# Expert weights as four rows to a partition, in 2 MB transfers, for thirteen of sixteen pairs of experts

## The chip, the cores and the metric

The kernel runs on one core of one Trainium2 chip. The metric is the device time of one execution in microseconds; lower is better.

## The reference

One step of a decoder layer in float32, for 256 prompt tokens and 8 sample tokens (264 in all), each 1024 wide: a gated recurrent mixer and a pooling mixer, then a mixture of 32 experts of which each token takes four, then a gated embedding and a final norm. The change touches the experts alone:

```
for each token: its 4 best experts e (router logits), with softmax weights
    gate = min(x @ w_gate[e] + b_gate[e], 7)          w_gate[e]: 1024 x 1024 float32, 4 MB
    up   = clip(x @ w_up[e] + b_up[e], -7, 7)         w_up[e]:   the same
    act  = (up + 1) * gate * sigmoid(1.702 * gate)
    y   += weight * (act @ w_down[e] + b_down[e])     w_down[e]: the same
```

All 32 experts are computed, so 96 matrices of 4 MB, 403 MB, are read from DRAM once.

## The kernel before

The core keeps everything in one SBUF tensor, `arena` (128 partitions), and uses the eight PSUM banks, `bank`. First come the mixers and the router (about 300 us), then the experts, two at a time in sixteen pairs, then the embedding gate and the output.

**Weights.** A matrix is read in four transfers of 1 MiB, called pieces here. Piece g holds rows 256g to 256g+255; `parts` (L425) gives partition p the rows 256g+2p and 256g+2p+1, which lie next to each other in DRAM, 8 KB in one run. A pair has 24 pieces: for each of gate, up and down (m = 0, 1, 2) and each step g = 0 to 3, one for each of the two experts. They go through a ring of 16 places in SBUF (`gran`). SyncE's queue (SP) issues them in the order in which they are used (`load_experts`, L445; the first two pairs in `load_first`, L437 and L439). Before each issue it waits on `s_used`, which TensorE raises when a piece is used up. TensorE waits for a piece on the semaphore of its place (`granules`).

**Rows of activations.** Since partition p holds rows 2p and 2p+1 of its 256, the other operand of a product must hold the same features on its partitions. Every second column is picked when the activations are turned: `every_other(k)` gives a slice with step 2, and with it `gather` (L1048, the prompt tokens), `gather_samples` (L1058) and `turn_half` (L1066) read their stationary operand. The gain of the norm is laid out the same way in `gffn`, made from a transposed copy of `g_ffn` at the job ("gf",), L753.

**Order of one pair on TensorE** (`pair`): the last gate step (g = 3); the up biases (L1158); the four up steps (L1142); the gather of the first half of the next pair's tokens (L1048, L1058); the turn of the activations (L1066) and of the combining matrix (L1213); the four down steps (L1142); the gather of the second half; the gate biases and the first three gate steps of the next pair (L1172); the mix of this pair's output into the token order (L1224). A step is 8 products of 128 rows by 64 columns with 512 moving columns. Each float32 product appears as two instructions in the trace, a transpose as one. So a step is 16 instructions, and a pair has 32 at L1048, 16 at L1058 and 8 at L1066. Pairs are counted from 0. In pair 14 the projection of the embeddings (L1077) is put between the up steps.

VectorE and ScalarE clip, gate and copy between these steps. The loop over pairs 2 to 13 is unrolled by two.

Of the kernel before, what the change touches and what calls it, by code (L numbers as in the profile page):

```python
# [14 lines left out]
P = 128  # L15
# [7 lines left out]
KD = D // P  # L23
# [86 lines left out]
def build(nc, x_prompt, x_sample, p_prompt, p_sample, state_hgrn, state_pool, g_mix, w_in,  # L110
# [14 lines left out]
    with ExitStack() as ctx:  # L125
# [40 lines left out]
        gain_rows = view(OG + 3 * P, P)  # L166
        lbt = view(take(32), 32)
# [5 lines left out]
        gffn = view(take(KD), KD)  # L173
        power = view(take(1), 1)
# [12 lines left out]
        def heads(start):  # L187
# [35 lines left out]
            "p (j n) -> p j n", j=2) for g in range(RING)]  # L223
        early = {7: view(TMP, GRAN).rearrange("p (j n) -> p j n", j=2),
# [80 lines left out]
        s_gr = [sem(f"granule{g}_loaded") for g in range(RING)]  # L305
        s_half = [sem(f"first_half_of_last_piece{n}_loaded") for n in range(2)]
# [104 lines left out]

        block = ctx.enter_context(nc.Block())
# [3 lines left out]
        def _(sp):  # L416
# [8 lines left out]
            parts = [w.rearrange("o e (g p j) n -> (o e) g p j n", j=2, p=P) for w in (w_gate, w_up, w_down)]  # L425
            ple = w_ple_gate[0].rearrange("(g j p) n -> g p j n", j=2, p=P)
# [14 lines left out]
            def load_experts(i, e, split=False):  # L441

                for at_ in range(2 * NGRAN * PER - (2 if split else 0)):
                    sp.wait_ge(s_used, 2 * NGRAN * i + at_ + 3)
                    sp.dma_start(gran[at_ % RING], source(at_, e)).then_inc(s_gr[at_ % RING], 16)  # L445
# [189 lines left out]
        def _(pe):  # L635
# [408 lines left out]
            def gather(ks, signal=None):  # L1044

                for k in ks:
                    for t in range(2):
                        ins = pe.matmul(XG[k // 4][:, (k % 4) * P:(k % 4 + 1) * P], h2[:, t, every_other(k)], oh[:, t, :],  # L1048
                                        start=(k % 4 == 0 and t == 0), stop=False, skip_group_check=True)
                        if signal and k % 4 == 0 and t == 0:  # L1050
                            ins.then_inc(signal, 1)

            def gather_samples(halves_=range(2)):
# [9 lines left out]
            def turn_half(out, src, c, signal=None):  # L1063
# [18 lines left out]
            def pair(i0, n, opening=False, second=False, last=False, project_tiles=False, alone=False):  # L1082

                i = i0 + n

                def granules(m, g, n=n):

                    for one in range(2):
                        at_ = 2 * NGRAN * n + 8 * m + 2 * g + one
                        if isinstance(i0, int) and i0 == 0 and at_ in early:  # L1090
                            pe.wait_ge(s_early[at_], 16)
                            yield early[at_]
                        elif isinstance(i0, int) and i0 == 0:
                            place = place_of(at_)
                            pe.wait_ge(s_gr[place], 16 if at_ <= 16 else 16 * ((at_ - 19) // RING + 2))
                            yield gran[place]
                        else:
                            pe.wait_ge(s_gr[at_ % RING], i0 * (16 * 2 * NGRAN // RING) + 16 * ((at_ - 19) // RING + 2))
                            yield gran[at_ % RING]

                def products(m, out, src, first, steps=range(4)):

                    for g in steps:
# [30 lines left out]
                        for j in range(2):  # L1134
# [3 lines left out]
                            for c in range(2):  # L1138
                                if halved and j == 1 and c == 1:
                                    ins.then_inc(s_yh, 1)  # L1140
                                for one in range(2):
# [4 lines left out]
                                    if m == 1 and k == 0 and c == 0 and one == 0:  # L1146
                                        ins.then_inc(s_used, 1)
                                    if j == 1 and c == 1 and not (g == 3 and one == 1):
                                        ins.then_inc(s_used, 1)
# [11 lines left out]
                def next_gate_steps():  # L1161

                    biases(range(2), i + 2)
                    for g in range(3):
                        if g != 1:
                            pe.wait_ge(s_xe, 2 * i + 3 + g // 2)
                        w = list(granules(0, g, n + 1))
# [1014 lines left out]
```

## Time and profile before

| | |
|---|---|
| device time, median of 3 runs | 1276.72 us (1275.2 to 1278.67) |
| the profiled execution's own time | 1274.7 us |
| its span, first to last instruction | 1273.0 us |
| mean granted TensorE clock | 0.998 of full speed |
| TensorE busy | 1242.8 us, 98% |
| weight loads of TensorE busy | 614.1 us, 48% |
| VectorE, ScalarE, GpSimd busy | 340.0, 172.5, 48.6 us |
| read from DRAM | 454.41 MB |

A busy engine is one that executes an instruction; TensorE's weight loads are counted apart from its products, since the two overlap. All views below are of one profiled execution, with times from the start of its span. A wait or a chain is put together from semaphore events.

### The profile page before, as it was taken

What the parts mean: (1) busy time and instruction counts of PE and PEld (TensorE: products, weight loads), DVE (VectorE), ACT (ScalarE), POOL (GpSimd) and SP (SyncE); (2) the same over time, 40 slices, a digit from 0 to 9 for tenths busy, and PEclk for the clock granted to TensorE, in tenths of its full rate; (3) what the DMA queues carried; (4) which work ended last, traced back from release to release, by engine and by line L of the source; (5) the groups of instructions that cost most, each with busy time, mean ns of one, the idle gap of its engine ahead of it and who ended that gap; (6) DMA issues with size and microseconds to landing.
All of it is one profiled execution on the core that took longest, in us unless ns stands there. A gap on an engine that the chain in (4) does not pass through costs nothing.

```text
span 1273.0 us, 15848 instructions
## 1 busy us (share of the span) xinstructions
PE 1242.8 (98%) x6326; PEld 614.1 (48%) x6326; DVE 340.0 (27%) x685; ACT 172.5 (14%) x434; POOL 48.6 (4%) x129
## 2 busy tenths in 40 slices
PE   9999999999999999999999999999999999999996
PEld 7857888855434344343434433333334343434343
DVE  3155445423131213122121303122121212121224
ACT  3136204011101010000001000000000010101013
POOL 2221000200000000000000000000000000000001
PEclk9999999999999999999999999999999999999999
DMA  9947713698999999999999999999999999999961
GB/s 347 287 143 261 273 67 97 238 354 355 417 409 415 422 421 422 420 422 421 422 422 422 422 422 422 422 422 422 422 421 422 422 422 422 422 422 420 421 241 36
DMA packets 79782, 460.98 MB, mean 362 GB/s; under 512 B 8158, under 2 KB 9235, under 8 KB 30842
## 3 DMA queue, kind: packets, MB, share of 16 engines
q1 hardware_dynamic: 74512, 445.18, 85.5%
q0 software_dynamic: 3280, 10.75, 2.7%
q10 hardware_dynamic: 1946, 4.43, 1.0%
q8 instruction: 31, 0.51, 0.2%
q14 instruction: 13, 0.11, 0.0%
HBM read 454.41 MB, written 6.39 MB: 362 GB/s over the span
## 4 chain that ended last, share of the span: by engine, by line
PE 78%; DMA 15%; SPq 5%; DVE 1%; issue 1%; ACT 0%; POOLq 0%; POOL 0%; DVEq 0%
PE bank L1142 29%; DMA arena<-in_w_gate_dram 10%; PE bank L1172 9%; PE bank L704 9%; PE bank L1224 5%; SPq L445 5%; PE bank L746 4%; PE bank L1048 3%; PE bank L685 2%; DMA arena<-in_w_down_dram 2%; DMA arena<-in_w_up_dram 2%; PE bank L1158 2%; PE bank L1058 2%; PE bank L1281 1%; PE bank L1299 1%; PE bank L896 1%
## 5 line engine op out<-in xcount | busy, mean ns | idle before, releaser
L1142 PE MATMUL bank<-arena 128*64 128x512 f32 x2352 | 520.3, 595 | 14.1 <-DMA arena<-in_w_up_dram 7.9
L1142 PEld LDWEIGHTS bank<-arena 128*64 128x64 f32 x2352 | 166.3, 137 | 349.3 <-issue 347.8
L1172 PE MATMUL bank<-arena 128*64 128x512 f32 x720 | 159.1, 595 | 1.0 <-DMA arena<-in_w_gate_dram 1.0
L2061 DVE TENSOR_TENSOR arena<-bank,arena 128x512 f32<-128x512 f32 (+1 forms) x92 | 59.0, 683 | 244.9 <-PE bank L1224 244.6
L704 PE MATMUL bank<-arena 128*128 128x264 f32 x512 | 115.9, 388 | 0.0
L704 PEld LDWEIGHTS bank<-arena 128*128 128x128 f32 x512 | 96.8, 190 | 16.6 <-issue 0.2
L1172 PEld LDWEIGHTS bank<-arena 128*64 128x64 f32 x720 | 51.1, 137 | 107.1 <-issue 107.1
L1048 PEld LDWEIGHTS bank<-arena 128*128 128x128 f32 x512 | 62.8, 196 | 25.4 <-issue 25.2
L1224 PE MATMUL bank<-arena 128*128 128x512 f32 (+1 forms) x192 | 75.0, 602 | 0.0
L2043 DVE TENSOR_SCALAR arena<-bank 128x512 f32<-128x512 f32 x32 | 20.6, 686 | 193.3 <-PE bank L1142 193.3
L2054 DVE COPY arena<-bank 128x512 f32<-128x512 f32 x16 | 11.1, 692 | 223.2 <-PE bank L1142 223.2
L1535 ACT ACTIVATE arena<-bank,arena 128x128 f32<-128x128 f32 x120 | 34.2, 368 | 265.0 <-PE bank L1058 265.0
L1048 PE MATMUL bank<-arena 128*128 128x128 f32 x512 | 68.9, 288 | 0.0
L746 PE MATMUL bank<-arena 128*128 128x264 f32 x256 | 57.2, 387 | 0.9 <-ACT arena L1414 0.9
L1547 ACT ACTIVATE arena<-arena 128x1024 f32<-128x1024 f32 x16 | 16.9, 1057 | 298.0 <-DVE arena L2023 298.0
L746 PEld LDWEIGHTS bank<-arena 128*128 128x128 f32 x256 | 48.6, 190 | 9.2 <-ACT arena L1414 1.0
L1224 PEld LDWEIGHTS bank<-arena 128*128 128x128 f32 (+1 forms) x192 | 24.5, 155 | 47.7 <-issue 47.1
L1158 PE MATMUL bank<-arena 32*128 32x512 f32 x128 | 40.4, 627 | 0.0
L1058 PE MATMUL bank<-arena 8*128 8x128 f32 x256 | 38.6, 290 | 0.0
L1567 ACT ACTIVATE arena<-bank 128x512 f32<-128x512 f32 x15 | 9.0, 597 | 210.3 <-PE bank L1142 210.3
L615 POOL TENSOR_SCALAR arena<-arena 128x1 f32<-128x1 f32 (+1 forms) x3 | 0.7, 217 | 944.7 <-ACT arena L1588 944.7
L1058 PEld LDWEIGHTS bank<-arena 8*128 8x128 f32 x256 | 32.5, 191 | 3.8
(264 smaller groups left out, 762.9 us busy)
## 6 DMA issues: line engine op xcount, KB each, us to landing
arena<-in_w_gate_dram SPq DMA_DIRECT2D x128, 1024.0 KB, 25.8
arena<-in_w_up_dram SPq DMA_DIRECT2D x128, 1024.0 KB, 26.0
arena<-in_w_down_dram SPq DMA_DIRECT2D x126, 1024.0 KB, 26.1
arena<-in_w_in_dram SPq DMA_DIRECT2D x14, 2048.0 KB, 11.0
out_dram<-arena POOLq DMA_DIRECT2D x9, 512.0 KB, 6.9
arena<-in_state_hgrn_dram POOLq DMA_DIRECT2D x8, 512.0 KB, 8.1
arena<-sample_values ACTq DMA_DIRECT2D x8, 512.0 KB, 8.9
arena<-in_w_out_dram SPq DMA_DIRECT2D x4, 1024.0 KB, 8.0
```

The costliest lines, as they stand in the source:

```text
L445: sp.dma_start(gran[at_ % RING], source(at_, e)).then_inc(s_gr[at_ % RING], 16)
L685: ins = pe.matmul(job_bank(name)[:, :], hT[:, k, toks(t)], w[:, k, :], start=(k == 0), stop=(k == KD - 1))
L704: ins = pe.matmul(job_bank(name)[:, 0:T], w[:, k, (c % 4) * P:(c % 4 + 1) * P], hT[:, k, :], start=(k == 0), stop=(k == KD - 1))
L746: ins = pe.matmul(job_bank((kind, h))[:, 0:T], w_slot[c % NSLOT][:, k, (h % 4) * P:(h % 4 + 1) * P], hT[:, k, :], start=(k == 0), stop=(k ...
L1048: ins = pe.matmul(XG[k // 4][:, (k % 4) * P:(k % 4 + 1) * P], h2[:, t, every_other(k)], oh[:, t, :], start=(k % 4 == 0 and t == 0), stop=F ...
L1058: ins = pe.matmul(XG[c][:, k * P:(k + 1) * P], h2[rows, 2, every_other(4 * c + k)], oh[rows, 2, :], start=False, stop=True, skip_group_che ...
L1142: ins = pe.matmul(out[c][hp(one), :], src[:, k * P + CAP * one:k * P + CAP * one + CAP], w[one][:, j, halves(c)], start=(first and k == 0) ...
L1158: pe.matmul((GATE + UP)[r][:, :], esel[rows], bias_gu[rows], start=True, stop=False, tile_position=(r * NE, 0))
L1172: ins = pe.matmul(GATE[c][hp(one), :], xT_e[:, k * P + CAP * one:k * P + CAP * one + CAP], w[one][:, j, halves(c)], start=False, stop=False)
L1224: return pe.matmul(out, comb[:, toks(t)], y_sb[:, halves(c)], start=True, stop=True)
L1535: ins = act.activation(xT_e[:, k * P:(k + 1) * P], bank[6 + c][:, (k % 4) * P:(k % 4 + 1) * P], ACT.Copy, scale=gffn[:, k:k + 1])
L2061: ins = dve.tensor_tensor(xs, src, xs, ALU.add)
```

## The change

For pairs 2 to 14 (the third to the fifteenth), a matrix is read in two transfers of 2 MiB. Partition p gets the rows 512G+4p to 512G+4p+3, 16 KB in one run of DRAM. Such a transfer fills two neighbouring places of the ring (`twin`), so there are eight of them, each with its own semaphore. The stream keeps its total and the order of matrices; within a matrix it is now half G of one expert, half G of the other. A transfer is issued when both places are used up, and TensorE raises `s_used` by 2 after every second step of an expert. Steps g = 0 and 1 read the two halves of one transfer, and so do g = 2 and 3.

The features on a partition change with it: for these pairs the gathers and the turn of the activations use a step of 4. The gain is kept a second time in that layout (`gffn_4`, from four more small transposes, one more copy and one more small load), and ScalarE scales with it. Pairs 0, 1 and 15 stay as they were; pair 1 gathers for pair 2 with step 4, pair 14 for pair 15 with step 2.

```diff
+        twin = [view(HG + (g - 4) * 2 * GRAN if 4 <= g < 6 else R + (g if g < 4 else g - 2) * 2 * GRAN, 2 * GRAN).rearrange(
+            "p (j n) -> p j n", j=4) for g in range(RING // 2)]
...
+            parts_4 = [w.rearrange("o e (g p j) n -> (o e) g p j n", j=4, p=P) for w in (w_gate, w_up, w_down)]
...
+            def load_twins(i, e, count):
+
+                for at_ in range(count):
+                    sp.wait_ge(s_used, 2 * NGRAN * i + 2 * at_ + 4)
+                    sp.dma_start(twin[at_ % (RING // 2)], parts_4[at_ // 4 % 3][e + 2 * (at_ // 12) + at_ % 2, at_ // 2 % 2])\
+                      .then_inc(s_twin[at_ % (RING // 2)], 16)
...
             with sp.Fori(1, PAIRS // PER - 1) as q:
-                load_experts(PER * q, 2 * PER * q)
-            load_experts(PAIRS - PER, NE - 2 * PER, split=True)
+                load_twins(PER * q, 2 * PER * q, NGRAN * PER)
+            load_twins(PAIRS - PER, NE - 2 * PER, NGRAN)
+            load_experts(PAIRS - PER, NE - 2 * PER, range(2 * NGRAN, 2 * NGRAN * PER - 2))
...
-            pe.wait_ge(ld["gffnr"], 16)
+            pe.wait_ge(ld["gffnr"], 32)
             begin(("gf",))
             for j in range(2):
                 pe.transpose(bank[5][:, 4 * j:4 * j + 4], gfin_rows[0:4, j:2 * P:2], ident[0:4, 0:4])
+            for j in range(4):
+                pe.transpose(bank[5][:, 32 + 2 * j:34 + 2 * j], gfin_rows_4[0:2, j:4 * P:4], ident[0:2, 0:2])
...
-            def every_other(k):
-                first = 2 * P * (k // 2) + k % 2
-                return slice(first, first + 2 * P - 1, 2)
+            def every_other(k, j=2):
+                first = j * P * (k // j) + k % j
+                return slice(first, first + j * (P - 1) + 1, j)
...
-                        ins = pe.matmul(XG[k // 4][:, (k % 4) * P:(k % 4 + 1) * P], h2[:, t, every_other(k)], oh[:, t, :],
+                        ins = pe.matmul(XG[k // 4][:, (k % 4) * P:(k % 4 + 1) * P], h2[:, t, every_other(k, j)], oh[:, t, :],
...
-                        ins = pe.matmul(XG[c][:, k * P:(k + 1) * P], h2[rows, 2, every_other(4 * c + k)], oh[rows, 2, :],
+                        ins = pe.matmul(XG[c][:, k * P:(k + 1) * P], h2[rows, 2, every_other(4 * c + k, j)], oh[rows, 2, :],
...
-                    ins = pe.transpose(out[c][:, j * P:(j + 1) * P], src[:, every_other(k)], ident)
+                    ins = pe.transpose(out[c][:, j * P:(j + 1) * P], src[:, every_other(k, step_)], ident)
...
+                        if twins:
+                            at_ = NGRAN * n + 4 * m + g // 2 * 2 + one
+                            pe.wait_ge(s_twin[at_ % (RING // 2)], i0 * (16 * 2 * NGRAN // RING) - 48 + 16 * (at_ // (RING // 2) + 1))
+                            yield twin[at_ % (RING // 2)][:, 2 * (g % 2):2 * (g % 2) + 2]
...
-                                    if j == 1 and c == 1 and not (g == 3 and one == 1):
-                                        ins.then_inc(s_used, 1)
+                                    if j == 1 and c == 1 and not (g == 3 and one == 1) and (g % 2 or not twins):
+                                        ins.then_inc(s_used, n_used)
...
-                    gather(range(4), s_used)
-                    gather_samples((0,))
+                    gather(range(4), s_used, n_used, next_apart)
+                    gather_samples((0,), next_apart)
...
-                    turn_half(AT, act_sb, c, s_used if last else None).then_inc(s_aT, 1)
+                    turn_half(AT, act_sb, c, s_used if last else None, rows_apart).then_inc(s_aT, 1)
...
             with pe.Fori(1, PAIRS // PER - 1) as q:
                 for n in range(PER):
-                    pair(PER * q, n)
-            pair(PAIRS - PER, 0, project_tiles=True)
+                    pair(PER * q, n, twins=True, next_twins=True)
+            pair(PAIRS - PER, 0, project_tiles=True, twins=True)
```

## Rows read from the trace of the kernel before

**Rows 1.** The page: busy shares, and the span in 40 equal slices.
```profile
PE 1242.8 (98%) x6326; PEld 614.1 (48%) x6326; DVE 340.0 (27%) x685; ACT 172.5 (14%) x434; POOL 48.6 (4%) x129
...
GB/s 347 287 143 261 273 67 97 238 354 355 417 409 415 422 421 422 420 422 421 422 422 422 422 422 422 422 422 422 422 421 422 422 422 422 422 422 420 421 241 36
```

**Rows 2.** The chain in order of time, one pair: start us, us, what.
```profile
600.01 1.06 PE bank L1158 x4
...
614.96 2.08 PE bank L1048 x16
617.04 1.14 PE bank L1058 x8
618.17 1.15 PE bank L1066 x8
...
637.66 10.45 PE bank L1172 x48
648.11 4.59 PE bank L1224 x12
652.70 3.58 PE bank L1142 x16
656.29 1.06 PE bank L1158 x4
```

**Rows 3.** The chain, marks of pairs 2, 8, 9 and 14, and the last wait.
```profile
431.19 1.06 PE bank L1158 x4
...
768.84 1.06 PE bank L1158 x4
...
828.30 1.06 PE bank L1158 x4
...
1114.64 3.65 PE bank L1172 x16
...
1126.47 1.06 PE bank L1158 x4
```

**Rows 4.** The waits of TensorE: us in total, times, longest us.
```profile
PE bank L1142 <- DMA arena<-in_w_up_dram: 7.9, 6, 1.3
PE bank L1142 <- DMA arena<-in_w_down_dram: 6.2, 6, 1.0
```

**Rows 5.** DMA packets of 16:24, 1218:1226 and 900:1000 us.
```profile
DMA packets 1673, 3.16 MB, mean 395 GB/s; under 512 B 149, under 2 KB 153, under 8 KB 1672
...
DMA packets 853, 3.28 MB, mean 410 GB/s; under 512 B 52, under 2 KB 52, under 8 KB 853
...
DMA packets 5796, 42.21 MB, mean 422 GB/s; under 512 B 644, under 2 KB 644, under 8 KB 644
```

**Rows 6.** The page, DMA issues: count, KB each, median us to landing.
```profile
arena<-in_w_gate_dram SPq DMA_DIRECT2D x128, 1024.0 KB, 25.8
```

**Rows 7.** Weight loads by form: count | busy us, mean ns of one | idle.
```profile
L704 PEld LDWEIGHTS bank<-arena 128*128 128x128 f32 x512 | 96.8, 190 | 16.6 <-issue 0.2
L1048 PEld LDWEIGHTS bank<-arena 128*128 128x128 f32 x512 | 62.8, 196 | 25.4 <-issue 25.2 <-DVE arena L1906 0.3
...
L1066 PEld LDWEIGHTS bank<-arena 128*128 128x128 f32 x128 | 16.5, 208 | 4.1 <-DVE arena L2049 2.3
...
L646 PEld LDWEIGHTS bank<-arena 128*128 128x128 f32 x32 | 3.5, 140 | 0.1
...
L1224 PEld LDWEIGHTS bank<-arena 128*8 128x8 f32 x64 | 1.7, 87 | 12.1 <-issue 12.1
```

**Rows 8.** Timeline of TensorE, 226.5 to 229 us: start us, us.
```profile
226.91 1.97 PE L646 MATMUL bank<-arena 128*128 128x128 f32 x16
228.71 0.61 PE L704 MATMUL bank<-arena 128*128 128x264 f32 x2
```

**Rows 9.** VectorE by form; L1945 and L1995 reduce with 128-byte steps.
```profile
L1945 DVE TENSOR_REDUCE arena<-arena 128x32 f32<-128x128 f32 x3 | 1.0, 372 | 0.1
L1995 DVE TENSOR_REDUCE arena<-arena 128x96 f32<-128x384 f32 x1 | 0.8, 820 | 0.0
...
L1994 DVE TENSOR_TENSOR arena<-arena 128x384 f32<-128x384 f32 x1 | 0.6, 557 | 0.0
```

More of the change, by code:

```diff
@@ L166, in build @@
         gain_rows = view(OG + 3 * P, P)
+        gfin_rows_4 = view(OG + 4 * P, 4 * P)
         lbt = view(take(32), 32)
@@ L173, in build @@
         gffn = view(take(KD), KD)
+        gffn_4 = view(take(KD), KD)
         power = view(take(1), 1)
@@ L305, in build @@
         s_gr = [sem(f"granule{g}_loaded") for g in range(RING)]
+        s_twin = [sem(f"two_places{g}_loaded") for g in range(RING // 2)]
         s_half = [sem(f"first_half_of_last_piece{n}_loaded") for n in range(2)]
@@ L410, in place_of @@
             return (at_ + (3 if at_ < 7 else 2)) % RING if at_ <= 16 else at_ % RING
+        first_loads = [sum(place_of(a) == g for a in range(2 * NGRAN * PER) if a not in early) for g in range(RING)]
+        last_loads = [sum(a % RING == g for a in range(2 * NGRAN, 2 * NGRAN * PER)) for g in range(RING)]
         block = ctx.enter_context(nc.Block())
@@ L439, in load_first, with load_experts @@
                     sp.dma_start(gran[place_of(at_)], source(at_, 0)).then_inc(s_gr[place_of(at_)], 16)
-            def load_experts(i, e, split=False):
-                for at_ in range(2 * NGRAN * PER - (2 if split else 0)):
+            def load_twins(i, e, count):
[3 more added lines that the diff above has]
+                      .then_inc(s_twin[at_ % (RING // 2)], 16)
+            def load_experts(i, e, ats=range(2 * NGRAN * PER)):
+                for at_ in ats:
                     sp.wait_ge(s_used, 2 * NGRAN * i + at_ + 3)
@@ L1080, in project, with pair, granules @@
                             fill_done(ins, ("pp" + r, t, j))
-            def pair(i0, n, opening=False, second=False, last=False, project_tiles=False, alone=False):
+            def pair(i0, n, opening=False, second=False, last=False, project_tiles=False, alone=False, twins=False,
+                     next_twins=False):
                 i = i0 + n
-                def granules(m, g, n=n):
+                rows_apart, next_apart = (4 if twins else 2), (4 if next_twins else 2)
+                n_used = 2 if twins else 1
+                def granules(m, g, n=n, twins=twins):
                     for one in range(2):
                         at_ = 2 * NGRAN * n + 8 * m + 2 * g + one
-                        if isinstance(i0, int) and i0 == 0 and at_ in early:
+                        if twins:
+                            at_ = NGRAN * n + 4 * m + g // 2 * 2 + one
+                            pe.wait_ge(s_twin[at_ % (RING // 2)], i0 * (16 * 2 * NGRAN // RING) - 48 + 16 * (at_ // (RING // 2) + 1))
+                            yield twin[at_ % (RING // 2)][:, 2 * (g % 2):2 * (g % 2) + 2]
+                        elif isinstance(i0, int) and i0 == 0 and at_ in early:
                             pe.wait_ge(s_early[at_], 16)
@@ L1166, in next_gate_steps @@
                             pe.wait_ge(s_xe, 2 * i + 3 + g // 2)
-                        w = list(granules(0, g, n + 1))
+                        w = list(granules(0, g, n + 1, next_twins))
                         for j in range(2):
@@ L1174, in next_gate_steps @@
                                                     w[one][:, j, halves(c)], start=False, stop=False)
-                                    if j == 1 and c == 1:
-                                        ins.then_inc(s_used, 1)
+                                    if j == 1 and c == 1 and (g % 2 or not next_twins):
+                                        ins.then_inc(s_used, 2 if next_twins else 1)
                 if opening:
@@ L1217, in pair @@
                 if not last:
-                    gather(range(4, KD), s_used)
-                    gather_samples((1,))
+                    gather(range(4, KD), s_used, n_used, next_apart)
+                    gather_samples((1,), next_apart)
                 def mix_half(t, c):
@@ L1331, in _ @@
             pair(0, 0, opening=True)
-            pair(0, 1, second=True)
+            pair(0, 1, second=True, next_twins=True)
             with pe.Fori(1, PAIRS // PER - 1) as q:
                 for n in range(PER):
-                    pair(PER * q, n)
-            pair(PAIRS - PER, 0, project_tiles=True)
+                    pair(PER * q, n, twins=True, next_twins=True)
+            pair(PAIRS - PER, 0, project_tiles=True, twins=True)
             pair(PAIRS - PER, 1, last=True)
@@ L1528, in _, with rows_in @@
             act.activation(exw, exw, ACT.Exp).then_inc(s_rta, 1)
-            def rows_in(i, c):
+            def rows_in(i, c, gain=gffn):
                 act.wait_ge(s_xg, 2 * i + c + 1)
@@ L1535, in rows_in @@
                     ins = act.activation(xT_e[:, k * P:(k + 1) * P], bank[6 + c][:, (k % 4) * P:(k % 4 + 1) * P], ACT.Copy,
-                                         scale=gffn[:, k:k + 1])
+                                         scale=gain[:, k:k + 1])
                 ins.then_inc(s_xe, 1)
@@ L1541, in projected, with pair @@
                 copy_out(name, pps[t][lanes(t), cols(t, n)], piece(name))
-            def pair(i, first=False, second=False, last=False, project_tiles=False):
+            def pair(i, first=False, second=False, last=False, project_tiles=False, next_gain=gffn):
                 if first:
@@ L1558, in pair @@
                 if not last:
-                    rows_in(i + 1, 0)
+                    rows_in(i + 1, 0, next_gain)
                 act.wait_ge(s_cT, i + 1)
@@ L1631, in _ @@
             pair(0, first=True)
-            pair(1, second=True)
+            pair(1, second=True, next_gain=gffn_4)
             with act.Fori(2, PAIRS - PER) as i:
-                pair(i)
+                pair(i, next_gain=gffn_4)
             pair(PAIRS - PER, project_tiles=True)
```

21 lines of the change are left out of this document (14 added, 7 removed).

## The prediction, before the changed kernel was run

> **What bounds the kernel now.** I read the page first: TensorE is busy for 98% of the span, and the DMA engines move 422 GB/s in nearly every slice from the fourteenth to the thirty-eighth [rows 1]. Two things that look full mean that the chain in order of time has to say which one is late. The reader is to see two regimes in it. In a pair in the middle of the span the chain holds TensorE work only, and from one pair's up biases (L1158) to the next it is 656.29 - 600.01 = 56.28 us [rows 2]. Those same marks stand at 431.19 for pair 2 and 768.84 for pair 8, six pairs at 56.27 us; then at 828.30, a step of 59.46, and so on to 1126.47 for pair 14 [rows 3]. A pair reads 24 pieces of 1 MiB, 25.17 MB; at 422 GB/s that is 59.63 us, so a piece lasts 2.485 us. DMA was always 3.4 us a pair slower than TensorE, TensorE ate up the lead that the loads had, and from pair 7 on it waits for weights. Had TensorE never waited, the twelve pairs from 431.19 to 1126.47 would take 12 x 56.27 = 675.2 us instead of 695.3: waits for weights cost 20.1 us in all. The list of waits names 14.1 us of them [rows 4]; the rest lies in gaps that it gives to nobody, and I use the distances of the marks. The last such wait ends at 1114.64, at the third gate step of pair 14 [rows 3], which needs that pair's first six pieces, number 342 of the stream counted from the first. From there to the end only TensorE and what follows it counts. So faster DMA can win at most 20.1 us, and every microsecond added to TensorE's 56.27 costs nothing while it is under 3.4 us a pair, and all of it above.
>
> **The change, part by part.** There are thirteen pairs (2 to 14) with 2 MiB transfers.
>
> *Longer rows.* A partition's run in DRAM grows from 8 KB to 16 KB. No row of before has a 16 KB run issued by SP, so I extrapolate: in three stretches the engines moved almost only 2 KB, 4 KB and 8 KB packets, at 395, 410 and 422 GB/s [rows 5]. Per packet and engine that is 2048 x 16 / 395 = 83 ns, 160 ns and 310.6 ns: about 75.4 ns per 2 KB and 9 ns that does not grow. A 16 KB packet then takes 310.6 + 301.6 = 612 ns, which is 428 GB/s and 2.449 us for 1 MiB, 0.036 us less than now. Between piece 48, the first of pair 2, and the 344 that the critical step will need lie 296 pieces: -10.7 us, if the loads set the end. The bounds are nothing, if a 16 KB run is cut in two, and 296 x 0.072 = -21.4 us if the whole fixed part went (301.6 ns for 8 KB, 2.413 us a piece), of which the loop can take up 20.1.
>
> *Coarser transfers.* The third gate step now waits for both experts' second transfers, so for eight pieces of its pair and not six: +2 x 2.485 = +5.0 us wherever the loads set the end. Places come free later too: the third gate step's pieces are now held over the mix (L1224, 4.59 us) and the last gate step (3.6 us), and the first of every two steps 3.5 us longer [rows 2]. That cannot empty the queue: a transfer lands 25.8 us after its issue now [rows 6], over ten pieces of backlog; less 8.2 + 3.5 us of later release and 5.0 us for the transfer itself, 9 us stay. I cost it at nothing; were that backlog not there, each later release would show as a gap in the loads.
>
> *Rows of activations four apart.* The weights of a partition are now rows 4p to 4p+3, so the gather (L1048, L1058) and the turn of the activations (L1066) take their stationary operand with a step of four floats, 16 bytes, instead of two. This is the part that is on TensorE's path in every pair: 32 + 16 + 8 instructions, with no cover but TensorE's own. What they cost now [rows 2]: 2.08 / 16 = 130 ns each, 142, and 1.15 / 8 = 144. Is a load bound by reading? The rows of weight loads [rows 7]: 8 columns take 87 ns, 128 adjacent columns 190 in a product and 140 in a transpose, with a step of two 196 and 208. So a column costs (140 - 87) / 120 = 0.44 ns when four share 16 bytes, and 1.01 ns when two do: 1.8 to 2.0 ns per 16 bytes either way. The spacing shows it: sixteen transposes of adjacent columns start 226.91 and are over by 228.71, 112 ns apart [rows 8], those with a step of two 144. With 196 and 208 ns loads the instructions come 130 and 144 ns apart, so the spacing is the load less some 65 ns. No TensorE row has a step of 16 bytes. VectorE has: its reduction over 128-byte steps takes 372 ns for 128 elements and 820 for 384, 1.75 ns an element, where an operation on 384 adjacent ones takes 557 [rows 9]. From below the price is nothing: if reading goes in units of 8 bytes, a step of two already pays one unit per column, and VectorE's 820 ns may be the work of closing 96 sums. From above it is 2.02 ns a column, twice the 1.01 of the transposes. I take twice the step of a strided product load, 2 x (196 - 87) / 120 = 1.82 ns, near the 1.75 of VectorE, as the nearest row: a load of 87 + 120 x 1.82 = 305 ns, a spacing of 240. That is +110 ns on 48 instructions and +96 on 8, 5.28 + 0.77 = 6.05 us a pair, 78.7 us for thirteen. TensorE's pair becomes 62.3 us, above the 59.6 that even the old load rate needs: the loads stop setting the end, their 20.1 us of waits go, and the two parts above no longer count.
>
> By the Trainium skill (Advanced Engine Details and Errata, section Memory Cachelines) SBUF has 16-byte lines, an access pays when each one goes to a new line, and two hits on a line absorb it; a step of two floats would be free and a step of four would pay. By that rule the sum is the one above. The trace agrees only in part: the loads of transposes are slower already at two hits, 208 ns against 140.
>
> *Small parts.* Four more transposes of gains at the ("gf",) job, in a stretch where TensorE has no idle time, at the same 0.24 us: +1.0. One more VectorE copy there and one more DMA on ScalarE's queue lie beside waits of those engines: 0. ScalarE only reads another gain: 0. SP issues half as many transfers, and nothing waits for SP alone: 0.
>
> **Sum.** -20.1 + 78.7 + 1.0 = +59.6 us. The profiled execution took 1274.7 us; the median of the runs is 1276.7, 2.0 above. 1274.7 + 59.6 + 2.0 = 1336 us.
>
> **The rivals.**
> A, the forecast, 0.66: a step of 16 bytes makes the loads slower than the cover. Its own range: with a load step only half dearer than now, 1.37 ns, the load is 251 ns, the spacing 186, 56 x 48 + 42 x 8 = 3.0 us a pair, +39.5 - 20.1 + 1.0 = +20, 1297 us; with 2.02 ns the load is 329 ns, the spacing 264, 7.4 us a pair, +77, 1354. Its range is 1297 to 1356.
> B, faster, 0.25: the wider step is free and the longer rows go at 428 GB/s. -10.7 + 5.0 + 1.0 = -4.7 us, 1272. For it speak the product loads, which a step of two hardly slowed (190 to 196). TensorE's own path is -20.1 + 1.0 + what the wider step adds, so B holds while that is under 14.4 us, 14.4 / 13 / 56 = 20 ns an instruction, and from 19.1 us, 26 ns, on the change is slower. At its best, -21.4 + 5.0 + 1.0 = -15.4, it gives 1261; I hold that for unlikely, since the three lengths show the fixed part at each.
> C, 0.09: the step is free and the long run is cut, or the engines gain nothing by it: 0 + 5.0 + 1.0 = +6, 1283. The change then doesn't do what it says. Against it stand the three packet lengths, which lie on one line.
>
> A measurement of this kernel tells a change from none at about 0.3%, 3.8 us. B lies at -0.37% and would fall on either side: 0.15 faster and 0.10 same; C 0.01 same and 0.08 slower; A slower. Faster 0.15, same 0.11, slower 0.74. The range must reach from A to B to leave out no more than two in ten: 1267 to 1356.
>
> **What would show it.** In the profile after: the weight loads of L1048, L1058 and L1066's successors near 305 ns instead of 196 to 208 (A), or as they are (B, C); sixteen gather instructions in 3.8 us instead of 2.08; the marks at the up biases 62.3 us apart through pair 14 with no wait for weights (A), or 56.3 at first and 58.8 later (B), or 59.6 (C); packets of 16 KB, the DMA rate down to about 404 GB/s (25.17 MB in 62.3 us) in A and up to 428 in B; the adjacent-column loads of other lines unchanged. The prediction is wrong if strided loads cost what they do now; it is off in size if their step is not near 1.82 ns.

## The result and the profile after

The changed kernel takes 1373.39 us (median of 4 runs, 1371.32 to 1377.8) against 1276.43 us before (median of the 4 runs beside it): ratio 1.0765, 95% interval 1.0738 to 1.0791. It is slower by 97 us. The forecast was 1336 us, and its range ended at 1356. It had the sign, and the slower weight loads came as forecast; a second loss, for which it had no term, carried the time past its range.

The page of the changed kernel, the lines that answer to [rows 1] and [rows 6]:

```profile
PE 1358.3 (99%) x6330; PEld 701.9 (51%) x6330; DVE 341.4 (25%) x686; ACT 172.5 (13%) x434; POOL 48.5 (4%) x129
...
GB/s 343 246 139 341 168 42 195 321 346 402 420 360 328 411 368 412 371 410 367 413 369 381 360 381 400 371 410 372 397 369 400 371 388 354 408 366 366 419 124 34
DMA packets 57321, 460.97 MB, mean 336 GB/s; under 512 B 5664, under 2 KB 6741, under 8 KB 28350
...
arena<-in_w_gate_dram SPq DMA_DIRECT2D x52, 2048.0 KB, 12.5
```

The DMA rate is no longer flat: the transfers now wait for places to come free, and a 2 MiB transfer lands 12.5 us after its issue, where half of that took 25.8. The packets fell from 79782 (on the page of the kernel before) to 57321. The run below with the same 2 MiB transfers in 8 KB runs has 77289, 19968 more, which is one for every second one of the 39936 8 KB runs of the thirteen pairs: a 16 KB run is one packet. The waits of TensorE name no weights at all. TensorE sets the time everywhere. One of its pairs, from the chain in order of time (start us, us, what), to be laid beside [rows 2]:

```profile
767.83 1.06 PE bank L1188 x4
768.88 13.88 PE bank L1172 x64
782.77 3.93 PE bank L1067 x16
786.70 2.06 PE bank L1077 x8
788.75 1.91 PE bank L1085 x8
790.66 0.63 PE bank L1243 x3
791.29 14.36 PE bank L1172 x64
805.65 3.93 PE bank L1067 x16
809.58 1.36 PE bank L1077 x5
810.94 0.23 PE bank L1188
811.17 0.23 PE bank L1077
811.41 1.09 PE bank L1188 x3
812.50 12.15 PE bank L1202 x48
824.65 4.59 PE bank L1254 x12
829.24 3.58 PE bank L1172 x16
832.83 1.06 PE bank L1188 x4
```

L1067 and L1077 are the gather (prompt tokens and sample tokens), L1085 the turn, L1243 the combining matrix, L1172 the up and down steps and the last gate step, L1202 the other gate steps, L1188 the biases, L1254 the mix. A pair takes 832.83 - 767.83 = 65.0 us (64.9 in most) where it took 56.3. The gather's sixteen instructions went from 2.08 to 3.93 us, as forecast (3.8). But the gate steps, whose operands nobody touched, went from 10.45 to 12.15 us, and the turning of the combining matrix from 0.37 to 0.63. The view by stretches shows why: the third figure from the end of each line is the granted TensorE clock as a share of full speed. The last line is from the kernel before.

```profile
core 0: us, PE busy (x) PEld busy (x) DVE busy (x) ACT busy (x) POOL busy (x), PEclk, DMA share, GB/s
782.77:788.00 5.23, 5.23 (x22) 5.11 (x22) 2.62 (x4) 0.00 (x0) 0.00 (x0) 1.00 0.98 420
788.00:790.00 2.00, 2.00 (x10) 1.88 (x10) 0.15 (x1) 1.14 (x4) 0.00 (x0) 0.70 1.05 451
790.00:792.00 2.00, 2.00 (x9) 1.16 (x9) 1.23 (x2) 0.39 (x1) 0.00 (x0) 0.50 1.03 442
...
805.65:812.50 6.85, 6.85 (x32) 5.97 (x32) 0.69 (x1) 1.42 (x5) 0.00 (x0) 1.00 0.99 426
812.50:816.00 3.50, 3.50 (x11) 1.09 (x12) 0.00 (x0) 0.32 (x2) 0.00 (x0) 0.53 1.04 445
...
600.00:700.00 100.00, 100.00 (x498) 41.71 (x498) 19.20 (x28) 8.65 (x22) 0.00 (x0) 1.00 1.01 422
```

Behind the first gather, and again behind the second, the clock falls and stands for a few microseconds at 0.5 of full speed, the lower of its two levels (1.2 of 2.4 GHz). The mean over the span fell from 0.998 to 0.959. Before, with the gather at 130 ns an instruction, it stood at 1.00 in every pair from 2 to 14.

### The profile page after: what moved, and what is told of

Its sections match the earlier page's. It is cut to its first block, busy times and chain, and to the rows that moved or that the text cites. A ratio compares the mean times of both kernels' runs of the same rounds, so it can differ in the third digit from the quotient of the medians.

```text
span 1371.5 us, 15403 instructions
## 1 busy us (share of the span) xinstructions
PE 1358.3 (99%) x6330; PEld 701.9 (51%) x6330; DVE 341.4 (25%) x686; ACT 172.5 (13%) x434; POOL 48.5 (4%) x129
## 4 chain that ended last, share of the span: by engine, by line
PE 98%; DVE 0%; ACT 0%; DMA 0%; issue 0%; POOLq 0%; POOL 0%; DVEq 0%
PE bank L1172 38%; PE bank L1202 13%; PE bank L721 8%; PE bank L1067 8%; PE bank L1254 5%; PE bank L763 4%; PE bank L1077 4%; PE bank L1188 3%; PE bank L1085 2%; PE bank L702 2%; PE bank L1311 1%; PE bank L1329 1%; PE bank L915 1%; PE bank L939 1%; PE bank L1243 1%; PE bank L1096 1%
## 5 line engine op out<-in xcount | busy, mean ns | idle before, releaser
L1172 PE MATMUL bank<-arena 128*64 128x512 f32 x2352 | 525.1, 602 | 0.0
L1172 PEld LDWEIGHTS bank<-arena 128*64 128x64 f32 x2352 | 165.1, 139 | 341.3 <-issue 339.8
L1202 PE MATMUL bank<-arena 128*64 128x512 f32 x720 | 180.6, 664 | 0.0
L1067 PEld LDWEIGHTS bank<-arena 128*128 128x128 f32 x512 | 110.8, 304 | 25.4 <-issue 25.1
L1202 PEld LDWEIGHTS bank<-arena 128*64 128x64 f32 x720 | 55.4, 151 | 124.9 <-issue 121.8
L1067 PE MATMUL bank<-arena 128*128 128x128 f32 x512 | 116.9, 382 | 0.0
L721 PEld LDWEIGHTS bank<-arena 128*128 128x128 f32 x512 | 96.8, 190 | 16.7 <-issue 0.2
L1254 PE MATMUL bank<-arena 128*128 128x512 f32 (+1 forms) x192 | 75.0, 602 | 0.0
L2087 DVE COPY arena<-bank 128x512 f32<-128x512 f32 x16 | 11.1, 692 | 229.6 <-PE bank L1172 229.6
L1077 PE MATMUL bank<-arena 8*128 8x128 f32 x256 | 63.4, 388 | 0.0
L1077 PEld LDWEIGHTS bank<-arena 8*128 8x128 f32 x256 | 56.5, 298 | 3.8
L763 PEld LDWEIGHTS bank<-arena 128*128 128x128 f32 x256 | 48.6, 190 | 9.1 <-ACT arena L1445 0.9
L1254 PEld LDWEIGHTS bank<-arena 128*128 128x128 f32 (+1 forms) x192 | 24.5, 155 | 47.7 <-issue 47.1
L1188 PE MATMUL bank<-arena 32*128 32x512 f32 x128 | 48.3, 654 | 0.0
L2085 DVE COPY arena<-bank 128x512 f32<-128x512 f32 x32 | 21.9, 691 | 63.2 <-PE bank L1085 63.2
## 6 DMA issues: line engine op xcount, KB each, us to landing
arena<-in_w_gate_dram SPq DMA_DIRECT2D x52, 2048.0 KB, 12.5
```

The lines of the kernel that those rows point to most:

```text
L721: ins = pe.matmul(job_bank(name)[:, 0:T], w[:, k, (c % 4) * P:(c % 4 + 1) * P], hT[:, k, :], start=(k == 0), stop=(k == KD - 1))
L763: ins = pe.matmul(job_bank((kind, h))[:, 0:T], w_slot[c % NSLOT][:, k, (h % 4) * P:(h % 4 + 1) * P], hT[:, k, :], start=(k == 0), stop=(k ...
L1172: ins = pe.matmul(out[c][hp(one), :], src[:, k * P + CAP * one:k * P + CAP * one + CAP], w[one][:, j, halves(c)], start=(first and k == 0) ...
L1188: pe.matmul((GATE + UP)[r][:, :], esel[rows], bias_gu[rows], start=True, stop=False, tile_position=(r * NE, 0))
L1202: ins = pe.matmul(GATE[c][hp(one), :], xT_e[:, k * P + CAP * one:k * P + CAP * one + CAP], w[one][:, j, halves(c)], start=False, stop=False)
L1254: return pe.matmul(out, comb[:, toks(t)], y_sb[:, halves(c)], start=True, stop=True)
```

## The experiments

The first three take the change apart.

**Step of four, old transfers.** From the kernel before:

```diff
-            pair(0, 1, second=True)
+            pair(0, 1, second=True, next_apart=4)
...
-                    pair(PER * q, n)
-            pair(PAIRS - PER, 0, project_tiles=True)
+                    pair(PER * q, n, apart=4, next_apart=4)
+            pair(PAIRS - PER, 0, project_tiles=True, apart=4)
```

> The kernel before with its 1 MiB transfers and 8 KB rows; only the gather and the turn of pairs 2 to 14 read their stationary operand with a step of four floats (so these pairs multiply features with the wrong weight rows). My theory: the whole loss is on TensorE (5.95 us a pair of slower loads, 2.7 us of lower granted clock), so the pair is 64.9 us, no wait for weights is left, and the time is that of the changed kernel less the 1 us of small parts, 1372 us. Rival: the 2 MiB transfers or the 16 KB rows slow TensorE's products as well; then the pair is 62.3 us and the time about 1336, or in between.

Measured: 1379.43 us, ratio 1.0798 (1.0779 to 1.0817), clock 0.959, gate steps 12.15 us, most pairs 64.9 us. The loss is there without one long transfer, 102 us beside 97, where 96 were expected. From pair 2 to pair 14 the mean pair is 65.4 us here and in the changed kernel, so the long transfers add nothing to it; of the 3.7 us between the two profiled spans, 2.8 lie ahead of pair 2.

**New transfers, step of two.** From the changed kernel:

```diff
-                rows_apart, next_apart = (4 if twins else 2), (4 if next_twins else 2)
+                rows_apart, next_apart = 2, 2
```

> The changed kernel with all its 2 MiB transfers, but the gather and the turn read with a step of two (wrong features again, same work). My theory: TensorE is back at 56.3 us a pair and the loads set the end: -10.7 us for the longer rows, +5.0 for the coarser transfers, +1.0 for the small parts, 1272 us, packets of 16 KB at 611 ns, marks 58.8 us apart in the later pairs. Rival C: the longer rows gain nothing, 1283. Rival of coarser transfers that empty the queue: above 1283, with gaps in the DMA rate.

Measured: 1270.92 us, ratio 0.9952 (0.9935 to 0.9970), clock 0.998. This is the case that rival B asked for, with a step that costs nothing, and B's sum was right in it: 6 us faster where the sum said 4.7. The page's rate and the marks of two late pairs in its chain:

```profile
GB/s 343 293 136 254 291 67 69 244 379 327 417 420 413 380 429 428 427 428 429 428 426 429 428 429 428 428 427 429 429 429 427 429 427 429 428 427 421 420 206 36
...
888.93 1.06 PE bank L1188 x4
947.66 1.06 PE bank L1188 x4
```

428 GB/s instead of 422, and 58.73 us a pair; the extrapolation from three packet lengths had said 428 and 58.8.

**The turn alone.** The first edit with `apart=4` and without `next_apart`.

> The kernel before, only the turn of the activations (8 instructions a pair) with a step of four in pairs 2 to 14. My theory: 8 x 0.1 = 0.8 us a pair more on TensorE, under the cover of 3.4 us that the loads give, so no change, 1276.4 within 0.3%, the waits for weights smaller by some 10 us in sum. Rival: each microsecond on TensorE counts, 13 x 0.8 = +10 us, 1287.

Measured: 1277.21 us, ratio 0.9996 (0.9986 to 1.0006). No change, but for another reason than mine: the eight instructions did not get slower.

```profile
561.97 1.16 PE bank L1066 x8
```

It was 1.15 in [rows 2]. So this run tests no cover, since there was nothing to cover. What the turn lost in the changed kernel, 1.15 to 1.91, lies in the stretch at the lower clock.

**The price of a step, measured by itself.** For each step, 12 products and 24 transposes ahead of the first gather, here those of the step of four:

```diff
+            for _ in range(12):
+                pe.matmul(bank[5][:, 0:P], h2[:, 0, slice(0, 509, 4)], ident, start=True, stop=True)
+            for _ in range(24):
+                pe.transpose(bank[5][:, 0:P], h2[:, 0, slice(0, 509, 4)], ident)
...
```

> The kernel before with 12 products (24 instructions) and 24 transposes put in ahead of the first gather for each step of 1, 2, 3, 4 and 8 floats in the stationary operand; their results are not used. My theory (a price per 16 bytes of SBUF touched, 1.8 to 2.0 ns): product loads of 190, 196, about 250, 305 and 305 ns. Rival (any step over 8 bytes pays one dearer access): 3 floats cost as much as 4, 305. Second rival (a price that grows with the step): 8 floats cost more than 4. If the low granted clock comes from slow loads, it falls in the runs of steps 4 and 8 only.

This was a single execution, and only what stands in its trace is read. The weight loads of that stretch by form (count | busy us, mean ns). L1328, L1332, L1336, L1340 and L1344 are the products with steps of 1, 2, 3, 4 and 8 floats, each line two below them the transposes with the same step:

```profile
L1344 PEld LDWEIGHTS bank<-arena 128*128 128x128 f32 x24 | 5.8, 334 | 0.0
L1340 PEld LDWEIGHTS bank<-arena 128*128 128x128 f32 x24 | 5.7, 328 | 0.0
L1336 PEld LDWEIGHTS bank<-arena 128*128 128x128 f32 x24 | 4.2, 261 | 0.0
L1342 PEld LDWEIGHTS bank<-arena 128*128 128x128 f32 x24 | 3.1, 212 | 0.0
L1334 PEld LDWEIGHTS bank<-arena 128*128 128x128 f32 x24 | 3.0, 208 | 0.0
L1332 PEld LDWEIGHTS bank<-arena 128*128 128x128 f32 x24 | 2.9, 196 | 0.0
L1338 PEld LDWEIGHTS bank<-arena 128*128 128x128 f32 x24 | 2.9, 200 | 0.0
L1346 PEld LDWEIGHTS bank<-arena 128*128 128x128 f32 x24 | 2.8, 191 | 0.0
L1328 PEld LDWEIGHTS bank<-arena 128*128 128x128 f32 x24 | 2.8, 192 | 0.3 <-DVE arena L1926 0.3
L1330 PEld LDWEIGHTS bank<-arena 128*128 128x128 f32 x24 | 2.7, 140 | 0.0
```

Products: 192, 196, 261, 328, 334 ns. Three floats cost between two and four, and eight hardly more than four: from a step of two on, the price goes by the 16-byte pieces touched. With steps of two, three and four floats 128 columns touch 64, 96 and 128 of them, and each 32 more cost 65 to 67 ns, about 2.1 ns a piece; the 32 more from adjacent columns to a step of two cost only 4 ns. That is the first theory with this exception, and it refutes both rivals for products. Transposes: 140, 208, 200, 212, 191. They pay once for not being adjacent and then nothing for width. The theory fails for them.

The clock in the 24 slow product instructions with the step of four:

```profile
313.06:318.66 5.60, 5.60 (x27) 5.60 (x26) 0.00 (x0) 0.00 (x0) 0.00 (x0) 1.00 0.00 0
```

It stayed at 1.00, and so it did in the transposes behind them and at the step of eight, so a run of slow loads over all partitions does not always bring it down. These runs differ from the gathers in more than one thing: no transfer was under way, and nothing but such loads and transposes stood around them.

By the Trainium skill (SBUF — State Buffer, section Door 1: The DMA port swizzle) an access that goes to a new 16-byte line pays, and four is given as the distance that four-byte elements can have for free. The product loads agree that the line is 16 bytes (196, 261, 328, 334 ns), but a step of four floats is already beyond what is free here, and so is one of three.

**The gathers spread out.** In pairs 2 to 13 a block of the gather is put behind each of the first three up and down steps:

```diff
+                        if spread and m and g < 3:
+                            gather_one(4 * (m - 1) + g)
...
```

> The changed kernel; in pairs 2 to 13 the gathers' instructions are the same, with the step of four, but three quarters of each gather are put one block at a time behind the first three up steps and the first three down steps, so slow loads come in stretches of 1.5 us instead of 6 to 8. My theory: the granted clock falls after long stretches of slow loads alone; spread, it stays at full speed at least in the second half of a pair, the pair is 62.3 to 63.6 us, and the time falls by 15 to 32 us, to 1341 to 1358. Rival: what follows a gather is slow for another reason (its own inputs, a full queue of loads); then the loss is the same or, with more places to pay it, larger: 1373 or more.

Measured: 1395.33 us, ratio 1.0928 (1.0906 to 1.0950). My number was wrong by 40 us and the time lies in the rival's range, though the clock of the second half of a pair did what my theory said: it stays at 1.00 from the second down step on, and the gate steps take 10.45 us again. The mean over the span is 0.983. From its chain:

```profile
728.93 3.63 PE bank L1193 x16
...
733.98 1.24 DVE arena L2111
...
735.26 1.61 PE bank L1085 x8
...
741.99 1.13 PE bank L1142 x4
...
760.75 10.45 PE bank L1225 x48
```

The gather had been the work that covers VectorE's clipping and product of the activations. Without it the turn starts at 735.26, 2.7 us after the up steps, and TensorE waits 0.96 us of that for VectorE. The clock then falls once, so that the turn takes 1.61 us and the first down step 4.50 instead of 3.58. And a block of four gather instructions takes 1.13 us instead of 4 x 0.246 = 0.98, one of the two sample instructions 0.66 for 0.46 to 0.51. So the pair is 67.6 us. I had priced neither the wait nor the shorter blocks. The run doesn't tell what brings the clock down, since the one fall that is left stands behind slow loads and behind a wait.

**The array fed during slow loads.** Moving operands of 256 columns wherever the step is four:

```diff
-                        ins = pe.matmul(XG[k // 4][:, (k % 4) * P:(k % 4 + 1) * P], h2[:, t, every_other(k, j)], oh[:, t, :],
+                        ins = pe.matmul(XG[k // 4][:, width(k, j)], h2[:, t, every_other(k, j)], oh[:, t:t + 2, :] if j == 4 else oh[:, t, :],
...
```

> The changed kernel; wherever the gathers read with the step of four, their moving operand has 256 columns instead of 128 (two tiles' selectors, so the gathered rows are wrong). The loads of the weights stay as slow and as long, but the array is fed for some 220 of the 246 ns between two of them instead of 110. My theory (the granted clock falls because the slow loads leave the array nearly idle): the clock stays full, the gate steps after the gather take 10.45 us again instead of 12.15, the turn 1.15 instead of 1.91, and the pair is 61.7 us, the time about 1328 us. Rival (the slow reads themselves, or the change of pace, bring the clock down): clock and time as in the changed kernel, 1373 us or a little more.

Measured: 1352.2 us, ratio 1.0591 (1.0576 to 1.0606), clock 0.984. Twice as many columns, and 21 us faster. Most pairs take 62.2 and 64.1 us in turn. By stretches (columns as above), one whole pair, and the one before it without its first 1.85 us; then the gate steps of both, from the chain:

```profile
759.27:821.52 62.25, 62.25 (x273) 28.41 (x273) 12.07 (x18) 4.33 (x11) 0.00 (x0) 1.00 0.98 404
697.00:759.27 62.27, 62.16 (x267) 29.01 (x263) 10.79 (x16) 3.88 (x11) 0.00 (x0) 0.97 0.96 400
...
738.96 12.13 PE bank L1207 x48
...
802.89 10.45 PE bank L1207 x48
```

In the first the clock holds at 1.00, the turn takes 1.16 us and the gate steps 10.45, with the weight loads as slow as ever (307 ns in the mean where the changed kernel has 304, a gather of 4.04 us). In the second the clock falls once, at the gate steps, not twice. So the slow loads by themselves are not enough to bring the clock down: with the same loads and more columns it falls once in two pairs instead of four times. This speaks for the theory that an array fed less while the loads are slow brings it down. It doesn't show how much feeding is enough, or why every second pair still has a fall; the time is 24 us over the 1328 expected.

**Which of the instructions.** The changed kernel with the step of four for one part of the gather only:

```diff
-                    gather_samples((0,), next_apart)
+                    gather_samples((0,), 2)
...
-                    gather_samples((1,), next_apart)
+                    gather_samples((1,), 2)
```

> The changed kernel, with the step of four for the 32 gather instructions over all partitions and the step of two for the 16 of the sample tokens (8 partitions each). Loads of the 32 cost 3.7 us a pair as in the changed kernel. If the clock falls because of the long run of slow loads alone, 2.7 to 3.4 us a pair come on top: a pair of 63 us, 1343 us. If the instructions that use 8 of 128 partitions are needed to bring it down, the clock stays full: a pair of 60.0 us, 1306 us.

```diff
-                    gather(range(4), s_used, n_used, next_apart)
+                    gather(range(4), s_used, n_used, 2)
...
-                    gather(range(4, KD), s_used, n_used, next_apart)
+                    gather(range(4, KD), s_used, n_used, 2)
```

> The other part: the step of four for the 16 instructions of the sample tokens alone. Their loads add 1.5 us a pair, TensorE's pair is 57.8 us, under the 58.8 us of the loads: no more than the run with the loads only, 1271 us, if the clock stays full; if the clock falls as in the changed kernel, the pair is 60.5 to 61 us and the time about 1312 us.

Measured: 1323.48 us, ratio 1.0366 (1.0349 to 1.0382), and 1319.96, ratio 1.0331 (1.0316 to 1.0346). One whole pair of the first, then of the second with its two falls, by stretches:

```profile
746.20:807.66 61.46, 61.46 (x273) 27.32 (x273) 12.17 (x18) 4.32 (x11) 0.00 (x0) 0.97 0.99 410
```

```profile
744.41:805.81 61.40, 61.40 (x273) 25.29 (x273) 12.07 (x18) 4.33 (x11) 0.00 (x0) 0.94 0.99 410
764.65:768.50 3.85, 3.85 (x14) 1.33 (x13) 0.85 (x2) 0.41 (x2) 0.00 (x0) 0.56 0.97 417
784.50:788.50 4.00, 4.00 (x12) 1.21 (x12) 0.00 (x0) 1.14 (x4) 0.00 (x0) 0.60 1.00 426
```

Two different ways to the same 61.4 us. The 32 instructions over all partitions cost 3.7 us of loads and one fall of the clock, behind the first gather: 61.46 - 56.27 - 3.70 = 1.5 us. Behind the second gather the gate steps take 10.45 us. The 16 of the samples, which use 8 partitions of 128, cost only 1.49 us themselves and 0.34 in the bias products that stand between them, which the transfers would have hidden, but the clock falls twice: 61.40 - 56.27 - 1.83 = 3.3 us. The first outcome lies between my two cases, the second is above the upper one (1312).

**Coarse transfers with the old rows.** Step of two, 2 MiB made of two runs of 8 KB to a partition:

```diff
-            parts_4 = [w.rearrange("o e (g p j) n -> (o e) g p j n", j=4, p=P) for w in (w_gate, w_up, w_down)]
+            parts_4 = [w.rearrange("o e (h g p j) n -> (o e) h p g j n", g=2, j=2, p=P) for w in (w_gate, w_up, w_down)]
...
-                rows_apart, next_apart = (4 if twins else 2), (4 if next_twins else 2)
+                rows_apart, next_apart = 2, 2
```

> The changed kernel with the step of two and with 2 MiB transfers that keep the 8 KB rows (two runs to a partition), right features. My theory: TensorE at 56.3 us a pair, no gain from rows, +5.0 us for the coarser wait and +1.0 for the small parts: 1282.4 us. Rival: the coarser transfer costs nothing, 1277.4, and then the longer rows alone make the difference of the run with both.

Measured: 1282.71 us, ratio 1.0053 (1.0035 to 1.0071): 5.6 us over the kernel before beside it, 6.0 expected. Against the run with new transfers and the step of two, the longer rows are worth about 12 us (10.7 expected).

**Adjacent reads.** The normalised rows are stored once in the gather's order, and all pairs use the layout of four:

```diff
+        def by_rows(a):
+            return a.rearrange("p (g j q) -> p g q j", j=4, q=P)
...
-                return parts[m][e + 2 * n + one, g]
+                return parts_4[m][e + 2 * n + one, g // 2][:, 2 * (g % 2):2 * (g % 2) + 2]
...
-                dve.tensor_scalar(h2[lanes(t), t, :], x[lanes(t), t, :], stat[lanes(t), 4 + t:5 + t], None,
+                dve.tensor_scalar(by_rows(h2[lanes(t), t, :]), in_rows(x[lanes(t), t, :]), stat[lanes(t), 4 + t:5 + t], None,
...
-                        ins = pe.matmul(XG[k // 4][:, (k % 4) * P:(k % 4 + 1) * P], h2[:, t, every_other(k, j)], oh[:, t, :],
+                        ins = pe.matmul(XG[k // 4][:, (k % 4) * P:(k % 4 + 1) * P], h2[:, t, k * P:(k + 1) * P], oh[:, t, :],
```

> The changed kernel's transfers, but the normalised rows are stored once in the order in which the gather wants them, so the gather's 48 instructions read adjacent columns; the turn of the activations keeps its step of four; all sixteen pairs use this layout, with 1 MiB transfers where the changed kernel has them. My theory: about 125 ns an instruction in the gather and 240 in the turn, 56.8 us a pair on TensorE, full clock, so the loads set the end: 1276.4 - 10.7 + 5.0 + 1.0 = 1272 us, faster than both kernels by a little. Rival: the turn's slow loads alone bring the clock down, one fall a pair of 1.7 us, still under the cover of 2.5 us: the same time; only if both parts come on top is it slower than before.

Measured: 1271.81 us, ratio 0.9966 (0.9952 to 0.9980), clock 0.997. The gather takes 1.98 us for sixteen. The time is as expected, a third of a per cent below the kernel before and about 100 us below the changed one. The turn was not slow (loads of 210 ns), as the run with the turn alone had shown, so TensorE's pair is 56.0 to 56.2 us and not 56.8.

**Adjacent reads in the turn too**, with VectorE writing the clipped sums in turned order:

```diff
-                    ins = pe.transpose(out[c][:, j * P:(j + 1) * P], src[:, every_other(k, step_)], ident)
+                    ins = pe.transpose(out[c][:, j * P:(j + 1) * P], src[:, k * P:(k + 1) * P], ident)
...
-                    ins = dve.tensor_scalar(u_sb[:, halves(c)], bank[2 + c][:, :], LIMIT, -LIMIT, ALU.min, ALU.max)
+                    ins = dve.tensor_scalar(turned_out(u_sb[:, halves(c)]), turned_in(bank[2 + c][:, :]), LIMIT, -LIMIT, ALU.min, ALU.max)
```

> As the run before, and VectorE also writes the clipped sums in turned order, so the turn of the activations reads adjacent columns as well. My theory: TensorE at 55.9 us a pair, the loads set the end, so again 1272 us: what it saves on TensorE hides behind the loads. Rival: VectorE's scattered writes are slower than 686 ns and TensorE waits for the activations; up to 2.5 us a pair of that would still be covered.

Measured: 1274.15 us, ratio 0.9975 (0.9960 to 0.9989). Not told apart from the run before it. The turn's loads fell from 210 to 146 ns, but TensorE now waits for VectorE in every pair, and where no weights are late its pair takes 56.3 to 56.5 us, more than without this edit. So the rival is seen, and the transfers cover it; among its waits:

```profile
PE bank L1214 <- DMA arena<-in_w_gate_dram: 9.8, 7, 1.6
PE bank L1097 <- DVE arena L2094: 7.9, 16, 2.4
```

**Fine transfers at the end.** The adjacent version with 2 MiB transfers for pairs 2 to 12 only:

```diff
-            load_twins(PAIRS - PER, NE - 2 * PER, NGRAN)
-            load_experts(PAIRS - PER, NE - 2 * PER, range(2 * NGRAN, 2 * NGRAN * PER - 2))
+            load_twins(PAIRS - 4, NE - 8, NGRAN)
+            load_experts(PAIRS - 4, NE - 8, range(2 * NGRAN, 2 * NGRAN * 4 - 2))
```

> The faster version with adjacent rows (e7), but with 2 MiB transfers for pairs 2 to 12 alone; pairs 13 and 14 are read in 1 MiB transfers of 8 KB rows. My theory: the third gate step of pair 14 then waits for six pieces of its pair and not eight, which gives back 5.0 us, less 30 pieces x 0.036 = 1.1 us of the rows' gain: about 3.7 us below the version with all of them, 1268 us. Rival: another wait of pairs 12 to 14 sets the end and the time stays at 1272.

Measured: 1267.08 us, ratio 0.9916 (0.9904 to 0.9928), the fastest of all. From its chain:

```profile
1081.07 27.59 DMA arena<-in_w_gate_dram
...
1108.79 3.65 PE bank L1208 x16
```

The last wait for weights ends at 1108.79; it was 1114.64 in [rows 3], and 1113.87 in the adjacent version with all transfers long. That is 5.1 us earlier than in that version, where the expectation had 3.7.

## Why the prediction was wrong

*The regime.* Right. The transfers set the end before, with 20.1 us of waits in all, and stop doing so once TensorE's pair is over 59.6 us. The changed kernel has no wait for weights. (The marks of [rows 3] put the first waits in pair 8, not 7; the sum doesn't use this.)

*Longer rows, coarser transfers.* Both sums were right, though neither counted in the changed kernel: one packet per 16 KB run, 428 GB/s and 58.7 us a pair; the coarse wait at +5.6 us together with the small parts. That the later release of places costs nothing held too: the rate is flat at 428 GB/s where the transfers set the pace.

*The step of four in the gather.* Right in mechanism, and in size partly by luck. The forecast had a load of 305 ns and a spacing 65 ns below it, 240. The loads with the step of four take 328 ns (the line's mean of 304 takes in three gathers of sixteen that kept the step of two and their 196), and the spacing is 3.93 / 16 = 246, 82 ns below: a load put too short and an overlap put too small nearly cancel. That gives (3.93 - 2.08) x 2 = 3.70 us for L1067 and, with 2.06 + 1.36 + 0.23 for L1077 against 1.14 + 0.78 + 0.24, 1.49 more: 5.19 us a pair where the forecast had 5.28. The bias products between the sample instructions take 0.23 + 1.09 us instead of 0.12 + 0.86, 0.34 more, for which the forecast had nothing. They do so in the pair of the wide operand whose clock holds at 1.00 too, so it is not the clock.

*The step of four in the turn.* Wrong: 0.77 us a pair were put there, and it costs nothing. I took transposes to pay like products, although their loads of 208 ns with a step of two were the one row that didn't fit. The 0.76 us that the turn did lose came from the clock.

*The step that failed* is "TensorE's pair becomes 62.3 us", a sum that adds only loads. It has no term for the granted clock: a fall of it was put at nothing, without a reason. The pair shown above takes 65.0 us: 56.3, 5.5 for the loads and the biases between them, and 3.2 for two stretches at half clock (0.76 in the turn, 0.26 in the combining matrix, 0.48 in the down steps, 1.70 in the gate steps). Most pairs take 64.93; thirteen pairs at 8.66 us more are 112.6; less the 20.1 of waits, 92.5. Most of the other 6 us up to the 98.5 between the two spans lies in two pairs with longer falls, from 699.93 and from 1092.46, which take 67.9 us each; from pair 2's mark at 440.29 to pair 14's at 1225.36 the mean pair is 65.4 us. The view by stretches of the kernel before showed a clock of 1.00 in every pair, and I carried that over to a kernel in which the gather's instructions follow one another at half the pace.

*The chances.* A came true, but its own range of 1297 to 1356 (its working ends at 1354) was too low, because it varied the price of a load and nothing else. B and C asked for a free step.

What stays open: why the sample instructions, a third of the gather with a sixteenth of its partitions, bring the clock down twice and the larger part once, and why the slow products in the run of steps did not. The runs differ in the partitions used, in what stands before and after and in the transfers beside them; no run varied those by themselves. That the step of four in the gather brings the clock down is shown, by the runs with it alone and without it; how it does so is not.

## What to carry to other kernels

Before a layout is changed for the sake of longer DMA rows, look at how the other operand is then read: here 12 us of better transfers were paid for with 48 wide-strided weight loads a pair. Store that operand once in the order in which it is read, and the transfers' gain remains. When instructions on TensorE get slower and not more numerous, ask what the granted clock will do in the stretch behind them: here work that the change doesn't touch paid for it.

## What the runs showed of the hardware that I had not expected

- A float32 product's load of 128 columns takes 192, 196, 261, 328 and 334 ns at steps of 1, 2, 3, 4 and 8 floats; a transpose's 140, 208, 200, 212 and 191. The two kinds of load have different prices for the same operand.
- Doubling the columns of the gather's moving operand made the kernel 21 us faster (1373.4 to 1352.2 us), since the clock fell less often (mean 0.984 against 0.959).
- Sixteen instructions a pair that use 8 of 128 partitions, slowed by 0.1 us each, cost 49 us (1320.0 against 1270.9 us). In TensorE's own pair that is 5.1 us, 1.8 of them for these instructions and the biases between them and 3.3 by the clock; the transfers hid a part of it.
